# GpSimd's low parts given to VectorE, rotary angles first, latent diagonals as four products, table B1 fetched earlier

## The reference

```python
h = rmsnorm(x, attn_norm_g)
z = h @ w_in      # a_q, a_k, a_v, i_q, i_k, i_w, c_q, c_kv, k_r, gates
# branch A: an index score picks 64 keys for each token, then attention with a relative bias
dots  = einsum('bqhd,bsd->bqhs', i_q, i_k) * 64 ** -0.5
score = where(causal, einsum('bqh,bqhs->bqs', i_w / 2, relu(dots)), -inf)
sel   = top_k(score, 64)
logits_a = a_q . a_k[sel] / 8 + rel_table[rel_bucket(pos_q - pos[sel])]
# branch B: latent attention with rotary parts
qb  = rmsnorm(c_q,  q_latent_norm_g)  @ w_uq      # 8 heads of 64 + 32 (rotary)
kvb = rmsnorm(c_kv, kv_latent_norm_g) @ w_ukv
ang = positions[..., None] * inv_freq             # cos and sin of it turn q_rope and k_r
logits_b = (q_nope . k_nope + q_rope . k_rope) * 96 ** -0.5, causal
```

## Time and profile before

| | us |
|---|---|
| median of 3 runs | 1009.25 (1009.16 to 1011.31) |
| profiled execution, whole | 1008.77 |
| its span, first to last instruction | 1007.0 |
| TensorE busy in it | 961.3 (95%) |
| VectorE busy | 666.0 (66%) |
| ScalarE busy | 552.3 (55%) |
| GpSimd busy | 160.1 (16%), of it low parts 32.7 |
| mean granted TensorE clock | 0.978 |

### The profile page before, as it was taken

How to read it: one execution, slowest core, us unless ns; L and a number is a source line. 1 busy time by engine, 2 the same in 40 slices (tenths; PEclk the granted TensorE clock), 3 DMA queues, 4 the chain that set the end, 5 groups by cost and what they waited for, 6 DMA issues and landing times.

```text
span 1007.0 us, 19387 instructions
## 1 busy us (share of the span) xinstructions
PE 961.3 (95%) x7816; PEld 926.9 (92%) x7816; DVE 666.0 (66%) x1441; ACT 552.3 (55%) x1106; POOL 160.1 (16%) x145
## 2 busy tenths in 40 slices
PE   8858899999999999999999999999897999999997
PEld 7758799999999999889999999999786999999997
DVE  5899664667555556686765566568898477555552
ACT  6536554465445455785644444458798365444434
POOL 2751100130000003001311111110000121111111
PEclk8979999999999999999999999999999999999999
DMA  8782624468545454322955555447311255555521
GB/s 290 196 189 89 189 84 155 181 185 260 184 172 199 173 178 177 107 85 106 285 208 195 179 174 201 170 171 255 120 44 43 84 210 172 197 176 177 200 85 42
DMA packets 26537, 165.82 MB, mean 165 GB/s; under 512 B 3352, under 2 KB 4248, under 8 KB 8016
## 3 DMA queue, kind: packets, MB, share of 16 engines
q1 hardware_dynamic: 24048, 156.61, 45.0%
q0 software_dynamic: 2400, 7.97, 4.2%
HBM read 161.03 MB, written 3.01 MB: 163 GB/s over the span
## 4 chain that ended last, share of the span: by engine, by line
PE 79%; DVE 11%; ACT 6%; issue 1%; DMA 1%; POOL 0%; SPq 0%; DVEq 0%; POOLq 0%; ACTq 0%
PE bank L524 12%; PE bank L528 12%; PE bank L532 11%; PE bank L561 9%; PE bank L565 9%; PE bank L563 9%; PE bank L536 3%; PE bank L535 3%; DVE lo L1616 2%; ACT PN L1324 2%; PE bank L541 2%; PE bank L539 2%; DVE DG L1874 1%; ACT hi L1092 1%; DVE PN L1950 1%
## 5 line engine op out<-in xcount | busy, mean ns | idle before, releaser
L1616 DVE TENSOR_TENSOR lo<-stage,hi 128x1024 fp32r<-128x1024 f32 x277 | 330.3, 1223 | 11.9 <-ACT hi L1092 11.8
L1092 ACT ACTIVATE hi<-stage 128x1024 fp32r<-128x1024 f32 x291 | 299.3, 1045 | 59.9 <-PE bank L565 52.3
L561 PE MATMUL bank<-UH,hi 128*128 128x256 f32 x608 | 172.3, 283 | 0.4 <-ACT UH L1394 0.4
L565 PE MATMUL bank<-UL,hi 128*128 128x256 f32 x608 | 172.2, 283 | 0.0
L563 PE MATMUL bank<-UH,lo 128*128 128x256 f32 x608 | 172.1, 283 | 0.0
L524 PE MATMUL bank<-HTH,hi 128*128 128x256 f32 (+1 forms) x1038 | 159.9, 290 | 9.6 <-DVE ZR L1705 4.1
L528 PE MATMUL bank<-HTH,lo 128*128 128x256 f32 (+1 forms) x1038 | 157.0, 288 | 0.5 <-DVE lo L1616 0.5
L532 PE MATMUL bank<-HTL,hi 128*128 128x256 f32 (+1 forms) x1038 | 156.7, 287 | 0.0
L524 PEld LDWEIGHTS bank<-HTH,hi 128*128 128x128 f32 (+1 forms) x1038 | 139.1, 193 | 14.8 <-issue 6.0
L532 PEld LDWEIGHTS bank<-HTL,hi 128*128 128x128 f32 (+1 forms) x1038 | 138.6, 193 | 3.1 <-issue 3.0
L528 PEld LDWEIGHTS bank<-HTH,lo 128*128 128x128 f32 (+1 forms) x1038 | 139.3, 194 | 2.0 <-issue 1.2
(11 more groups left out here) (309 smaller groups left out, 1480.4 us busy)
## 6 DMA issues: line engine op xcount, KB each, us to landing
stage<-in_stream SPq DMA_DIRECT2D x144, 1024.0 KB, 4.8
BT<-scratch POOLq DMA_DIRECT2D x8, 256.0 KB, 16.1
BT<-scratch POOLq DMA_DIRECT2D x4, 512.0 KB, 18.4
stage<-in_stream SPq DMA_DIRECT2D x3, 512.0 KB, 9.3
scratch<-VR POOLq DMA_DIRECT2D x2, 768.0 KB, 21.0
XT<-in_xt SPq DMA_DIRECT2D x4, 256.0 KB, 6.0
B<-scratch POOLq DMA_DIRECT2D x4, 256.0 KB, 5.0
out<-ROWS SPq DMA_DIRECT2D x4, 256.0 KB, 2.4
```

The lines of the kernel that those rows point to most:

```text
L561: e.matmul(out, hi[:, j % HI_SLOTS, c:c + 128], rows.high(k), start=start and n % 2 == 0, stop=False)
L565: last = e.matmul(out, hi[:, j % HI_SLOTS, c:c + 128], rows.low(k), start=False, stop=stop)
L1092: e.activation(hi[:, j % HI_SLOTS, 0:w], stage[:, j // 2 % ST_PAIRS, j % 2, 0:w], ACT.Copy).then_inc(*up("hi", ("hi", j, 0)))
L1616: e.tensor_tensor(lo[x], stage[x], f32(hi[:, j % HI_SLOTS, 0:sched[j][2]]), ALU.subtract).then_inc(*up("lo", ("lo", j, 0)))
```

## The change

1. GpSimd makes no low parts: `LO_BY_POOL` goes, VectorE's `low_split` makes those of slabs 6 to 19 at their places in its program. GpSimd's program is left with sums of squares, branch sums, SiLU scaling, tables and copies, in the order of before.
2. POSR is the second load, with a semaphore of its own; posq goes ahead of idc. The angle steps stand ahead of and between the first low rows: 8, 3, 1, 2 and the rest ahead of low part 2.
3. DG is four products 128x128 with one column each.
4. GpSimd fetches B1 as soon as the index scores are made (and "table sent" is there), without waiting for the mask. VectorE makes the flag between ckv and slab 8, ahead of cq 0, instead of in p = 1.

```diff
-    HI_BY_DVE = set()
-    LO_BY_POOL = set(range(6, 20))
@@ def low_split(j), vector
-            if j in LO_BY_POOL:
-                return
@@ vector, start
+        q.wait_ge(*at("columns"))
+        some_angle(8)
         for k in range(2):
             low_row(rows, k, gain(0, k))
         first_half(0)
         for k in range(2, 4):
             low_row(rows, k, gain(0, k))
+        some_angle(3)
         first_half(1)
+        some_angle(1)
         for k in range(4, 8):
             low_row(rows, k, gain(0, k))
+        some_angle(2)
         low_split(1)
         slabs.begin(2)
         slabs.splits(1)
+        some_angle(99)
         slabs.flush()
         last_squares(SQ, "in", 0)
@@ vector, after avw
         slabs.splits(1)
-        some_angle(5)
         slabs.give(one_tile("ckv", 0))
-        some_angle(5)
+        q.wait_ge(*at("follows"))
+        e.tensor_reduce(flag[:, 0:1], NB[0:1, 0:255], AX.X, ALU.min)...
+        e.tensor_scalar(flag[:, 0:1], flag[:, 0:1], -1.0, 1.0, ALU.mult, ALU.add)...
+        e.tensor_copy(flagi[:, 0:1], flag[:, 0:1])...
         slabs.splits(2)
         slabs.give(one_tile("cq", 0))
-        some_angle(99)
@@ vector, latent roots
-        e.tensor_tensor(DG[:, :, :], idc[:, 0:128].unsqueeze(1).to_broadcast([128, 4, 128]), fc.unsqueeze(2).to_broadcast([128, 4, 128]), ALU.mult)
+        for c in range(4):
+            e.tensor_scalar(DG[:, c, :], idc[:, 0:128], fc[:, c:c + 1], None, ALU.mult)
@@ gpsimd (the calls of Splits and its low_split go everywhere)
+        sum_squares("in")
-        q.wait_ge(*at("positions"))
+        q.wait_ge(*at("positions in rows"))
         e.tensor_tensor(NI[0:1, 0:255], ...)
         ...
-            if p == 2:
-                q.wait_ge(*at("mask"))
+        for o in range(2):
+            q.wait_ge(*at("score", o, 3))
+        toeplitz(B1[:, :, 0:256], 0, 8, 0, 256, "bias")
+        toeplitz(B1[:, :, 256:384], 0, 8, 128, 128, "bias", ("b1 loaded",))
+        q.wait_ge(*at("flag", 2))
+        ...
+        choose()
@@ sync
         load(col[:, :], io["columns"], "columns", ("columns",))
+        load(POSR[:, :], ..., "positions", ("positions in rows",))
         load_half(0)
         ...
+        load(posq[:, :], io["posq"], "columns2", ("positions",))
         load(idc[:, :], io["cst"], "masks", ("masks",))
         load_pair(2)
-        load(POSR[:, :], ..., "positions")
-        load(posq[:, :], io["posq"], "positions", ("positions",))
         load_pair(3)
```

More of the change, by code:

```diff
@@ L162 @@
     "hi", "high", "square", "root", "key", "query", "latent", "relu", "gate", "exp", "pt",
-    "lo", "hi_dve", "low", "high_dve", "sums_dve", "x", "root_dve", "z", "top", "probabilities", "key_dve", "query_dve", "step",
-    "lo_pool", "sums", "pool_step", "branch", "silu",
+    "lo", "low", "high_dve", "sums_dve", "x", "root_dve", "z", "top", "probabilities", "key_dve", "query_dve", "step",
+    "sums", "pool_step", "branch", "silu",
     "w0", "w1", "w2", "w3", "w4", "w5", "wone2", "wfirst0", "wfirst1", "x0", "x1", "x2", "x3", "columns", "masks",
-    "positions", "tables", "scratch", "keys", "bias", "bias2", "bias3", "compress", "out",
+    "positions", "columns2", "tables", "scratch", "keys", "bias", "bias2", "bias3", "compress", "out",
 )
@@ L1815, in some_angle, with low_half, both_low @@
                 pass
+        q.wait_ge(*at("columns"))
+        some_angle(8)
+        for k in range(2):
+            low_row(rows, k, gain(0, k))
+        first_half(0)
+        for k in range(2, 4):
+            low_row(rows, k, gain(0, k))
+        some_angle(3)
+        first_half(1)
+        some_angle(1)
+        for k in range(4, 8):
+            low_row(rows, k, gain(0, k))
+        some_angle(2)
+        low_split(1)
+        slabs.begin(2)
+        slabs.splits(1)
+        some_angle(99)
+        slabs.flush()
+        last_squares(SQ, "in", 0)
+        slabs.splits(1)
+        q.wait_ge(*at("columns"))
+        e.tensor_tensor(g23[:, :], col[:, 16:24], col[:, 24:32], ALU.mult).then_inc(*up("step", ("g23",)))
+        e.tensor_scalar(bgh[:, :], col[:, 75:91], 0.5, None, ALU.mult).then_inc(*up("step", ("gate bias",)))
+        def low_half(name, src, here, there, out, high, scale):
+            q.wait_ge(*at(*name, 0))
+            for n, rows_ in enumerate((here, there)):
+                x = e.scalar_tensor_tensor(out[rows_], src[here], scale, f32(high[here]), ALU.mult, ALU.subtract)
+                if n:
+                    x.then_inc(*up("key_dve", name + (1,)))
+        def both_low(name, src, own, outs, scale):
+            low_half(name, src, slice(64 * own, 64 * own + 64), slice(64 - 64 * own, 128 - 64 * own), outs[1], outs[0], scale)
         def iq_low(i):
@@ L2312, in add_square, with sum_squares @@
             e.tensor_tensor(sq[:, 0, :], sq[:, 0, :], sq[:, k, :], ALU.add).then_inc(*up("sums", ("squares so far", stage, c, k), *[("squares", stage, c, 0)] * (k == 5)))
[L2314 to L2349, removed]
+        def sum_squares(stage, both=False):
+            for k in range(8):
+                add_square(SQ, k, stage, 0)
+                if both:
+                    add_square(SQ2, k, stage, 1)
         def toeplitz(out, which, heads_, first, n, port, *keys):
@@ L2582, in sync @@
         load(col[:, :], io["columns"], "columns", ("columns",))
+        load(POSR[:, :], bass.AP(io["positions"].tensor, 0, [[0, 128], [1, 256]]), "positions", ("positions in rows",))
         load_half(0)
```

189 lines of the change are left out of this document (24 added, 165 removed).

## The result

The changed kernel takes 1001.86 us (median of 4 runs, 1001.13 to 1003.15) against 1009.91 of before on the same chip (1009.16 to 1011.31): ratio 0.992, 95% interval 0.9903 to 0.9937. It is 8.0 us faster; 14.7 was forecast, and 1001.86 lies above the range's 1001.5. The profiled execution is the longest of the four: 1003.15 us, span 1001.3, granted clock 0.984, TensorE busy 959.7, VectorE 662.4, ScalarE 552.6, GpSimd 127.0.

The account below looks back on a forecast made before the run. TensorE, busy 813 of 832 us from 175 us on, leaves gains only in the opening, where it waits for VectorE. Terms 9.9 - 0.5 - 0.7 + 6.0 = 14.7 us off 1008.77 give 994.1, median 994.5; range 989.5 to 1001.5.

Parts of the forecast that it names:

- The stall and its cause: VectorE's DG near 46 us: 13.88 us, laid to GpSimd's low parts; four products take 0.9 us, VectorE gains 13.0.
- Rival 4: VectorE's long rows come from the transfers, not GpSimd; DG keeps 13.0 us, kernel slower, 1013.7 us; chance 0.04.
- Front: Opening to 45 us, with POSR and angle steps moved: lead 0.4 us, bounds -1.8 and +0.75.
- Low parts 6 to 15: On VectorE around DG: 6 to 12 cost nothing; 13 to 15 behind DG give back 3.4 us.
- Transfers: Scratch writes and rotated-key copies ahead of the first logits at about 61.5 us: 0.5 us lost, bounds 0 and 3.
- Rival 1: Scratch writes become the bound: tables or rotated key land 3 to 5 us after need; 997.5 to 999.5 us; chance 0.10.
- The wait at 93.79: TensorE's wait for VectorE's ZR stays, grows to 2.0 us and fixes the lead at 9.9; 0.7 us charged.
- B1: Early fetch of table B1 removes TensorE's idle of 1.03 and 2.49 us and 2.5 of slow products: 6.0 us.
- The sum: Whole kernel: 9.9 - 0.5 - 0.7 + 6.0 = 14.7 us faster.

Follow-up runs that it names:

- before_nopool: The kernel before the change with VectorE making all low parts and GpSimd none, nothing else changed: 1008.72 us, ratio 0.9992.
- before_pause: The kernel before the change with one wait added: GpSimd pauses after low part 12 until DG is made: 1009.4 us, ratio 1.0003.
- before_dg4: The kernel before the change with only DG made as four one-input products, GpSimd still making its low parts: 1009.67 us, ratio 1.0006.
- late_scratch: The changed kernel with two of the three scratch writes moved behind the rotated key's copies and B1's reads: 995.14 us, ratio 0.9858.
- pair9_late: The changed kernel with SyncE issuing the two rotated-key copies ahead of weight pair 9 instead of behind it: 996.95 us, ratio 0.9874.

## Why the prediction came out half right

**The stall and its cause.** Right. DG's 13.88 us were the doing of GpSimd's low parts: before_nopool 0.69, after 0.87. Rival 4 (transfers) is refuted by the DMA share of 0.99 beside the short DG. The rule of the Trainium skill that had been weighed (SBUF — State Buffer, Who interferes with whom), a lock for one whole instruction, fits the other long rows, those of the scores in before_pause too, but not DG: in before_dg4 a one-input product waits through the last six instructions of the run, and in before_pause a two-input one through the last three. Why DG alone is passed over stays open.

**Front.** The term was +0.4 with bounds -1.8 and +0.75. g0's ZR starts at 45.33 against 43.92: -1.4, inside the bounds and at their bad end. That is one pair of executions: the same tile starts at 42.8 to 46.8 us in three other kernels with the old opening and at 44.3 to 44.9 in five others with the new one, so how much of the -1.4 is the change's own is not shown. POSR landed in 3.1 us, as taken, and the eight steps were done at 7.3. But the last five steps took 0.71 to 0.97 us beside the sums of squares where the steps before them took 0.29 to 0.43 alone, and low part 2 was ready at 22.5, behind the 21.7 given as its worst: TensorE waited 1.50 us (0.99 to 1.51 in the six profiled kernels with this opening).

**Low parts 6 to 15.** Low 6 to 12 cost nothing, as said: VectorE idled 2.77 us ahead of g0. The waits behind them were 2.65 for the latents and 0.89 for the keys, against 1 to 2.5 forecast. Without the copies the first logits could have started at 70.47 - 7.43 = 63.04, against 61.5; the front was 1.8 us behind its term and more than covers the 1.5 us.

**Transfers: the step that failed.** "I take 0.5 us lost, bounds 0 and 3." It was 7.43 us of waiting. The eight products behind the wait also ran at the lower of the clock's two levels (granted 0.50 from 70 to 74 us): 2.55 us from 70.47 to 73.02, in late_scratch 1.30 at 1.00. Little of that was left at the gate tile, which starts 22.7 us behind the first logits in after and 22.5 in late_scratch. Two things went wrong. The argument "everything starts 6 us earlier too" let the scratch writes and the key move together; in fact the writes moved from 40.7 to 37.05, 3.7 us, and the key's copies from 64.0 to 54.7, 9.3 us. Before, they were issued when the writes were nearly over and took 4.3 to 4.9 us; after, in the midst of them, and behind a pair 9 that the writes had held up (pair9_late: 4.9 of the 7.43 us). And of the earlier trace rows the 21.1 us of pair 9 were read as a place in the queue ("62 to 65"), without asking what moves beside the writes: from 40 to 55 us the trace of before lists no packet of the hardware queue at all, and 1.29 MB of the software queue's. The last copy landed at 55.5 + 14.9 = 70.4. Rival 1 had the mechanism, with 3 to 5 us where it was 7.4.

**The wait at 93.79.** Forecast to grow from 1.03 to 2.0; it was 3.28 in after and 2.38 in late_scratch. VectorE is nearer to the bound there than the sum had it.

**B1.** Right: 6.1 us between the landmarks against 6.0, no wait for GpSimd, no slow stretch (clock 1.00 from 110 to 130 us). The first logits with B1 need the flag at 110.9; it was signalled at 88.9. These logits were forecast for 99 to 101 us; they are later by the lead that was lost. The reads landed 10.3 to 16.1 us after issue and cost nothing by their slack.

**The sum.** In the two profiled executions: DG 13.0 and front -1.4; 8.3 would have been left at the first logits, so that -3.3 falls to low parts and latents (forecast -3.4); copies -7.4, so 0.9; at the gate tile 0.6; B1 +6.1, so 6.7, and 8.0 in the medians. With the writes moved, 14.3 (late_scratch), against the 14.7 forecast.

## What to carry to other kernels

When a stall goes, the work behind it moves, and the large transfers beside it do not, or not by as much: list the small transfer that the next stage needs, the time at which it will now be issued, and what the DMA engines are doing at that time, not at its old one. A large write with slack belongs behind a small copy without any. If two transfers move by different amounts, their old landing times say little: the key's copies landed 4.3 to 4.9 us after issue before and 6.7 and 14.9 after.

## What the runs showed of the hardware that was not expected

**While the software queue wrote the tables, the hardware queue moved almost nothing.** The queues from 40 to 55 us (packets, MB, share of the 16 engines; q0 is GpSimd's, q1 SyncE's), in after:

```profile
q0 software_dynamic: 432, 1.56, 95.8%
q1 hardware_dynamic: 19, 0.11, 1.8%
```

And in late_scratch:

```profile
q1 hardware_dynamic: 144, 1.05, 20.0%
q0 software_dynamic: 68, 0.26, 15.4%
```

One weight pair of 1 MB is issued in this stretch in both: beside three scratch writes it took 21.1 us to land, beside the tail of one 4.8. The Trainium skill (DMA: Bandwidth & Descriptors, Queues, rings and completion order) has each engine take the queues in turn, a packet from each; 432 packets against 19 is not that, or the hardware queue's packets were not there to be taken, which the runs don't tell apart.

**The issue itself grows.** The two key copies took 0.73 and 3.58 us to issue in after, 0.60 and 0.73 in late_scratch, at the same time beside the same work of VectorE. In pair9_late, with the scratch writes but no load ahead of them, they took 0.73 and 4.63, so it is not the load pair in front that draws the issue out.

**Beside a run of GpSimd's low parts VectorE's instructions wait in two ways.** DG waited for the end of the run and not of one instruction: 13.88, 13.43 and 5.57 us, each ending 0.1 to 0.6 us after the last low part. The score rows of before_pause (2.46, 2.59, 2.42 us), the second IK half (done at 30.1 us, in the midst of a run that ends at 31.8) and the probability products (4.41 us for two beside two low parts) were each let in after one. It is not the number of inputs (before_dg4 and the probability products have one, DG and the score rows two) nor the load on the DMA engines (their share is 0.96 beside DG and 0.97 beside the score rows of before_pause). What it is the runs do not show. So a price of one GpSimd instruction for each meeting is a lower bound, and the rest of the run has been seen.
